# A float32 transformer stack on one core: launch order, last ffn with stationary weights, final norm's gain stored early, two mixer ends reordered

## What is computed

```python
for l in range(DEPTH):
    h = rms_norm(x, norm1_g[l]); proj = h @ w_in[l]          # 1024 -> 3584
    ...
    x = x + jnp.concatenate([ret, sb], axis=-1) @ w_out[l]
    h = rms_norm(x, norm2_g[l])
    x = x + (jax.nn.silu(h @ w_gate[l]) * (h @ w_up[l])) @ w_down[l]   # 2816 wide
return rms_norm(x, final_g)
```

```python
def ffn_sublayer(s, mod, j, g_pre, g_post, wg, wu, wd):
    y = adaln_in(s, g_pre, mod[..., 3 * j, :, :], mod[..., 3 * j + 1, :, :])
    return adaln_out(s, swiglu(y, wg, wu, wd), g_post, mod[..., 3 * j + 2, :, :], FFN_RES)
```

## Time and profile before

| | |
|---|---|
| median of 3 runs | 2390.13 us (2389.59 to 2390.61) |
| the profiled execution | 2390.28 us |
| its span, first to last instruction | 2388.2 us |
| TensorE busy | 2326.7 us, 97% |
| VectorE, ScalarE, GpSimd busy | 1437.3, 1024.8, 166.5 us |
| mean granted clock of TensorE | 0.993 |
| DMA | 364.31 MB, 153 GB/s |

### The profile page before, as it was taken

How to read it: one execution, slowest core, us unless ns; L and a number is a source line. 1 busy time by engine, 2 the same in 40 slices (tenths; PEclk the granted TensorE clock), 3 DMA queues, 4 the chain that set the end, 5 groups by cost and what they waited for, 6 DMA issues and landing times. The chain is left out here.

```text
span 2388.2 us, 28840 instructions
## 1 busy us (share of the span) xinstructions
PE 2326.7 (97%) x10860; PEld 1887.3 (79%) x10860; DVE 1437.3 (60%) x2175; ACT 1024.8 (43%) x1771; POOL 166.5 (7%) x205
## 2 busy tenths in 40 slices
PE   8999999999999999999999999999999999998998
PEld 7877788777888888877777788887878887776777
DVE  5677765777676733455757674337766346466455
ACT  6554556544632223355545222235222235465444
POOL 1200003000000000022100000001000001410000
PEclk9999999999999999999999999999999999999999
DMA  6556654377555522332114554223676232323554
GB/s 223 180 198 242 227 180 156 112 272 254 188 195 184 185 97 80 106 90 71 53 54 167 203 200 145 89 92 118 219 242 204 87 106 81 114 71 104 193 179 141
DMA packets 119880, 364.31 MB, mean 153 GB/s; under 512 B 12224, under 2 KB 12864, under 8 KB 119744
## 3 DMA queue, kind: packets, MB, share of 16 engines
q1 hardware_dynamic: 117488, 355.62, 43.6%
q0 software_dynamic: 2256, 6.86, 1.2%
HBM read 361.35 MB, written 1.09 MB: 152 GB/s over the span
## 5 line engine op out<-in xcount | busy, mean ns | idle before, releaser
L1763 DVE TENSOR_TENSOR wlo<-raw,whi 128x1024 fp32r<-128x1024 f32 x524 | 643.8, 1233 | 483.3 <-ACT whi L1185 476.8
L1185 ACT CAST whi<-raw 128x1024 fp32r<-128x1024 f32 x524 | 548.7, 1051 | 562.0 <-PE ps L632 547.4
L632 PE MATMUL ps<-whi,xhi 128*128 128x512 f32 x1136 | 463.1, 408 | 8.7 <-ACT xhi L1225 4.5
L632 PE MATMUL ps<-wlo,xhi 128*128 128x512 f32 x1136 | 446.6, 393 | 0.0
L632 PE MATMUL ps<-xhi,whi 128*128 128x512 f32 x960 | 375.7, 391 | 1.4 <-DVE hid L2104 1.4
L632 PE MATMUL ps<-whi,ahi 128*128 128x512 f32 x952 | 375.1, 394 | 1.3 <-DVE wlo L1763 0.8
L632 PE MATMUL ps<-xhi,wlo 128*128 128x512 f32 x960 | 373.7, 389 | 0.0
L632 PE MATMUL ps<-xlo,whi 128*128 128x512 f32 x960 | 373.6, 389 | 0.0
L632 PE MATMUL ps<-wlo,ahi 128*128 128x512 f32 x952 | 372.3, 391 | 0.0
L632 PE MATMUL ps<-whi,xlo 128*128 128x512 f32 x1136 | 338.1, 393 | 0.7 <-DVE xlo L1857 0.7
L632 PE MATMUL ps<-whi,alo 128*128 128x512 f32 x952 | 277.3, 390 | 0.0
(11 more groups left out here) (172 smaller groups left out, 1659.4 us busy)
## 6 DMA issues: line engine op xcount, KB each, us to landing
raw<-in_w SPq DMA_DIRECT2D x524, 512.0 KB, 3.5
mraw<-in_w_mod SPq DMA_DIRECT2D x144, 512.0 KB, 5.0
grow<-gains POOLq DMA_DIRECT2D x11, 512.0 KB, 7.3
x<-in_x SPq DMA_DIRECT2D x2, 512.0 KB, 5.2
x<-in_ctx SPq DMA_DIRECT2D x1, 1024.0 KB, 5.7
out<-x SPq DMA_DIRECT2D x2, 512.0 KB, 2.6
rmask<-in_rmask SPq DMA_DIRECT2D x1, 768.0 KB, 5.3
ws<-in_ws POOLq DMA_DIRECT2D x2, 256.0 KB, 11.8
```

Of the source, the lines that this page charges most:

```text
L632: return nc.tensor.matmul(o, lhsT, rhs, start=start, stop=stop, skip_group_check=True)
L1185: nc.scalar.copy(whi[:, slot, :], raw[:, slot, :]).then_inc(hi_done, 1)
L1763: nc.vector.tensor_tensor(wlo[:, slot, :], raw[:, slot, :], whi[:, slot, :].bitcast(F32), ALU.subtract).then_inc(w_split, 1)
```

## The change

- Launch: TensorE runs nine products of 128 columns on the `ones` tile into bank 7 before it waits for the identity (`warm`), and four after tile 0's transposes. VectorE splits unit 0 before it waits for identity and columns. ScalarE makes the operand of tile 0 right after its square and casts unit 1 between its halves, units 2 and 3 after it, then turns to tile 1.
- Last ffn (sublayer 9): chunks 1 to 10 go across, with 256 activation columns moving. Gate and up part of a pair share one bank of four (`pair_place`).
- Final norm: SP stores the gain column behind the load of unit 16; POOL only loads the row in sublayer 3. VectorE's waits on `gains_stored` count one store less, and one stays only for the second block.
- First block's mixers: `o_copied` and `z_taken` are waited for first, six products on `ones` follow, then the wait for `mix_ready`.
- Mixer 5's end: VectorE's output(19) and output(20) ahead of maxima(22) and maxima(23); the copies of mixed rows (`mix_out2`) ahead of the last weights and exponentials; TensorE's `lead_units` 2 and 3 of the second LEAD tile ahead of gmlp.
- Turn 8 to 9 (`ends_whole`): all tall units first, five products on `ones`, tile 0's transposes, seven more. VectorE and ScalarE sum and square tile 1 ahead of and between the operand's parts; ScalarE norms tile 1's row.

```diff
...
-    return s["kind"] == "ffn" and s["tw"] == 4 and c > 0
+    return s["kind"] == "ffn" and (s["tw"] == 4 or s["i"] == 9) and c > 0
...
+        def pair_place(s, q, part):
+            if s["tw"] == 2:
+                return bank((2, 3, 6, 7)[q % 4], 256 * part, 256 * part + 256)
+            return bank(pair_banks(q)[part])
...
             return s["i"] == 2 * DEPTH - 1 and g == CTX_GROUP
+        def ends_whole(s):
+            return s["kind"] == "mix" and s["tt"] == 2
...
                 count += len(SUBS[s["i"] + 1]["wide"][st])
+                count -= s["tt"] == 4 and st == TRAIL
                 RSTD_AT[s["i"] + 1, st] = count
...
+        GAINS_AT = 16
+        final_stored = sem("final_stored")
         X_AT, count = {}, 0
...
                     load_mod(u - 26)
+                if u == GAINS_AT:
+                    sp.wait_ge(cols_landed, 16)
+                    sp.dma_start(gains[0].rearrange("(k p) -> p k", p=P), cols[:, C_FINAL, :],
+                                 allow_slow_non_contiguous=True).then_inc(final_stored, 16)
                 load_mods(u)
...
                 return nc.tensor.matmul(o, lhsT, rhs, start=start, stop=stop, skip_group_check=True)
+            def warm(times, b):
+                for _ in range(times):
+                    mm(bank(b, 0, P), ones[:, :], ones[:, :], True, True)
...
                             q = 2 * (c - 1) + pair
-                            if k == 0 and q >= 3:
+                            if s["tw"] == 2:
+                                if k == 0 and q >= 4:
+                                    pe.wait_ge(pair_taken, s["pair0"] + q - 3)
+                            elif k == 0 and q >= 3:
                                 pe.wait_ge(pair_taken, s["pair0"] + q - 2)
...
                                 pe.wait_ge(chunk_taken, LEAD4 + TAKEN[s["i"], 0, TRAIL])
-                            for part, b in enumerate(pair_banks(q)):
+                            for part in range(2):
                                 c0 = CH * kk + 256 * part + P * pair
                                 hi, lo = (w[:, slot, c0:c0 + P] for w in (whi, wlo))
-                                mm(bank(b), hi, xhi[:, k, :], k == 0, False)
-                                mm(bank(b), hi, xlo[:, k, :], False, False)
-                                last = mm(bank(b), lo, xhi[:, k, :], False, k == KD - 1)
+                                o, xh, xl = pair_place(s, q, part), xhi[:, k, 0:P * s["tw"]], xlo[:, k, 0:P * s["tw"]]
+                                mm(o, hi, xh, k == 0 and (part == 0 or s["tw"] == 4), False)
+                                mm(o, hi, xl, False, False)
+                                last = mm(o, lo, xh, False, k == KD - 1)
                             if k == KD - 1 and pair == 0:
...
                             transposes_in(s, LEAD)
+                            warm(4, 7)
                         wide_pass(s, c, st)
...
                     pe.wait_ge(chunk_taken, LEAD4 + TAKEN[s["i"], s["chunks"] - 1, st])
-                    if across(s):
+                    if across(s) and s["tw"] == 4:
                         pe.wait_ge(pair_taken, s["pair0"] + 2 * s["chunks"] - 3 + st)
...
                             transposes_in(nxt, LEAD)
-                    elif nxt is not None and st == TRAIL and k == s["k"] - 4 + before_the_end(nxt):
+                    elif nxt is not None and not ends_whole(s) and st == TRAIL and k == s["k"] - 4 + before_the_end(nxt):
                         transposes_in(nxt, LEAD)
...
                         tall_pass(s, nxt, g, st)
+                if ends_whole(s):
+                    warm(5, 7)
+                    transposes_in(nxt, LEAD)
+                    warm(7, 7)
...
                     else:
-                        pe.wait_ge(mix_ready, n["mix"] + 4)
                         pe.wait_ge(o_copied, 8 * l + 8)
...
                         b = b0 + pair
+                        if pair == 0:
+                            warm(6, b)
+                        pe.wait_ge(mix_ready, n["mix"] + 4)
                     for kk in range(2):
...
                         if j == 25:
+                            lead_units(s, 1, (2, 3))
                             gmlp(s, (0, 1), 4)
-                            lead_units(s, 1, (2, 3))
                         if j == 26:
...
+            pe.wait_ge(dve_link, 2)
+            warm(9, 7)
             pe.wait_ge(ident_landed, 16)
...
                     high4(1, f_act, s["f_act0"][st] + 1)
+                    if trail:
+                        square_x(1, X_AT[trail["i"], 1])
+                        split_hi(s["u_wide"] + 3)
+                        act.wait_ge(rstd_ready, RSTD_AT[s["i"], TRAIL])
+                        nc.scalar.activation(rows[:, 1, :], x[:, 1, :], ACT.Copy, scale=rstd[:, 1:2]).then_inc(xn_ready, 1)
+                        n["tr"] += 2
+                        return
+                elif launch:
+                    high4(0, f_ready, s["f0"][st] + 1)
+                    split_hi(s["u_wide"] + 1)
+                    high4(1, f_ready, s["f0"][st] + 2)
+                    n["tr"] += 2
+                    return
                 else:
...
                     return
+                if s is not None and ends_whole(s):
+                    if st == LEAD:
+                        square_y(s, LEAD)
+                        split_hi(nxt["u_wide"])
+                        split_hi(nxt["u_wide"] + 1)
+                        square_x(0, X_AT[s["i"], 0])
+                        square_y(s, TRAIL)
+                    operand_hi(nxt, st, s if st == LEAD else None)
+                    return
                 if s is not None and s["blk"] == 2:
...
                     if st == LEAD:
-                        split_hi(1)
+                        operand_hi(nxt, st, launch=True)
+                        split_hi(2)
+                        split_hi(3)
+                        return
                 elif s["i"] == 2 * DEPTH - 1:
...
                     act.wait_ge(pair_taken, s["pair0"] + q - 1)
-                nc.scalar.activation(pgate[:, pair, :], bank(pair_banks(q)[0]), ACT.Silu).then_inc(pair_silu, 1)
+                nc.scalar.activation(pgate[:, pair, 0:P * s["tw"]], pair_place(s, q, 0), ACT.Silu).then_inc(pair_silu, 1)
...
                     proj_out(s, columns, TRAIL)
+                if mixed is not None:
+                    act.wait_ge(tr_ready, mixed)
+                    mix_out2(s, LEAD, 2, 3)
                 if j < len(jobs):
...
                     step2(s, 22)
-                    step2(s, 23)
-                    act.wait_ge(tr_ready, tr + 2)
-                    mix_out2(s, LEAD, 2, 3)
+                    step2(s, 23, mixed=tr + 2)
                     act.wait_ge(mixT_dve, dve_out + 1)
...
                     last.then_inc(f_ready, 1)
+                    if trail:
+                        add_tile(trail, TRAIL, 0)
                     low4(0)
...
                         split_lo(s["u_wide"] + 1)
+                    if trail:
+                        mean_square(1)
+                        n["rstd"] += 1
                     dve.wait_ge(f_act, s["f_act0"][st] + 1)
...
                     which = c_n1(s["l"]) if s["kind"] == "ret" else c_n2(s["l"])
+                    if launch:
+                        split_lo(s["u_wide"])
+                        dve.wait_ge(ident_landed, 16)
+                        dve.wait_ge(cols_landed, 16)
                     for b in range(2):
...
                                                 ALU.mult).then_inc(f_ready, 1)
-                    if launch:
-                        split_lo(s["u_wide"])
                     low4(0)
...
                     if h == 0:
+                        if between:
+                            normed_tile(s, LEAD, 0)
...
                         split_lo(first)
+                    operand_lo(nxt, st, s if st == LEAD else None)
+                    return
+                if s is not None and ends_whole(s):
+                    if st == LEAD:
+                        out_tile(s, LEAD, 0)
+                        add_tile(s, LEAD, 0)
+                        split_lo(first)
+                        mean_square(0)
+                        out_tile(s, TRAIL, 0, between=True)
                     operand_lo(nxt, st, s if st == LEAD else None)
...
                 dve.wait_ge(pair_silu, s["pair0"] + q + 1)
-                nc.vector.tensor_tensor(hid[:, 2 * c + pair, :], pgate[:, pair, :], bank(pair_banks(q)[1]),
+                nc.vector.tensor_tensor(hid[:, 2 * c + pair, 0:P * s["tw"]], pgate[:, pair, 0:P * s["tw"]], pair_place(s, q, 1),
                                         ALU.mult).then_inc(pair_taken, 1)
...
-                        dve.wait_ge(gains_stored, 16 * n["g"])
+                        if s["blk"] == 2:
+                            dve.wait_ge(gains_stored, 16 * (n["g"] - 1))
                         dve.wait_ge(mod_taken, sum(u < nxt["u_wide"] for u in COLS_AT))
...
```

(27 more changed lines are left out.)

## The result

The changed kernel took a median of **2371.94 us** over 6 runs (2371.59 to 2372.63), against 2390.12 over 6 runs of the kernel before beside it: a ratio of 0.9926, interval 0.9917 to 0.9936. That is 18.2 us faster, where 25.9 were forecast. The time lies at the upper end of the stated range of 2358 to 2372: the median is just inside it, and 0.9926 of the 2390.13 us of the kernel before, 2372.4, is 0.4 outside. The profiled execution took 2371.8 us.

The account below looks back on a forecast made before the run. TensorE was taken as the bound, busy 2326.7 of 2388.2 us. Terms 2.0 + 3.4 + 5.5 + 2.6 + 6.5 + 5.9 = 25.9 came off 2390.3, giving 2364.4 us; range 2358 to 2372.

Parts of the forecast that it names:

- Final norm's row: Second layer's ffn: moving the gain store off POOL removes TensorE's 3.8 us `hrow` wait and 1.7 of half clock; 5.5 us.
- first mixer's end: Mixer 5: outputs ahead of maxima give 0.8, weight units ahead of gmlp fill 1.75 us idle; 2.6 us, bounds 0.8 and 3.9.
- turn: Mixer 8 to last ffn: reordering starts the second stream at 2191.7 instead of 2198.33; 6.5 us, bounds 4.5 and 8.
- Last ffn: Sublayer 9's ten chunks: stationary weights with 256-wide products take 110.8 us instead of 116.65; 5.9 us, bounds 7.3 and 1.1.
- I take 0.115, near the half: Last ffn: assumed step in us of a 256-wide product with its weight load, between bounds 0.114 and 0.12.
- rival 2: Last ffn: the 256-wide step is 0.12, or new waits cost as much; 4.8 us lost, 2369.2; chance 0.13.
- Dummy products: First block's mixed rows: six dummies fill 0.7 us of each stall, preventing half clock behind, 2 x 1.7; 3.4 us.
- rival 1: Mixed rows, launch, turn: dummies do not hold the clock; loses 3.4, 0.8 and 1.7 us, 2370.3; chance 0.17.
- Launch: Kernel start: earlier split starts the first product 1.2 us sooner, dummies give 0.8; 2.0 us, bounds 1.2 and 3.4.
- I cost it at nothing: Launch layer, units 17 to 19: loads behind the moved store cost 0, as casts wait for TensorE; uncovered, up to 5.5.
- rival 3: Launch layer: the early store stalls it as it did the later one; 5.5 us lost, 2369.9; chance 0.10.
- 0.4 off: Turn to last ffn: POOL's gain store comes 6 us earlier and falls on chunk 1's loads, costing 0.4 us.

Follow-up runs that it names:

- the old turn alone: Changed kernel with the old order of the turn to the last ffn, stationary weights kept there: 2378.17 us, ratio 0.9953.
- the repaired version: Changed kernel with gain store behind unit 31, ScalarE's lambda exponential behind chunk 1's first splits, fifth tall unit cast and split earlier in retention layers: 2368.39 us.
- its twin without dummies: The repaired version without the six dummy products ahead of the first block's mixed rows, those at launch and turn kept: 2372.18 us, ratio 0.9925.
- the second profile: The changed kernel measured again without any edit, as baseline of a later series: 2372.41 us, ratio 0.9927.

## Why the prediction missed

- **Final norm's row, first mixer's end, turn: right, with some luck in the sizes.** 5.3 for 5.5, 2.7 for 2.6, 6.7 for 6.5. Undoing the first mixer's edits cost the same 2.7, but its gain by positions was 1.1 in the profile with 10.2 us of half clock. The turn's end came where its chain was worked out; TensorE waits there 0.9 us for a split and 0.9 for a cast, and not at all for tile 1's row.
- **Last ffn: the step that failed is "I take 0.115, near the half".** Half of 0.2275 holds half of the fixed part, but each product pays all of it, 0.013 us, and 480 more products pay it 480 more times: 6.2 us, most of the 7.5 that the removed gate transposes were to give. The argument offered for 0.115 (each step of a pair holds two loads and two products) was wrong: the 0.12 of the only 256-column row of the trace was the number to take, and would have given 115.6 us. This was rival 2, priced at 4.8 lost; 4.4 were.
- **Dummy products: the clock held with them** (1.00 behind both mixed rows in each of the ten profiles that have them there; a step of 0.23 at launch), so rival 1 falls. The ground given was off, though: they fill 1.5 us and not 0.7, and no run shows whether a stall with 1.2 us left would have held. Nor is a short idle time enough by itself: in mixer 5 of two profiles (the old turn alone, and the three repairs) the clock fell at 1187 and 1183 behind idle times of 0.4, 0.6 and 0.4 us. The 1.7 us that rival 1 put on the turn's dummies were nothing. The failed step is that the 1.7 us behind each stall would reach the end. The forecast did not ask what TensorE would need 1.7 us earlier: the fifth tall unit, cast behind ScalarE's copies. The forecast named the next late thing at the turn, and not here. Measured 0.95 for 3.4; shown by the repaired version and by its twin without dummies.
- **Launch: 2.6 gained by the 13th product for a forecast 2.0**, then 1.0 given back at unit 4. Same omission.
- **Early store: "I cost it at nothing" was wrong**, rival 3 partly right. Unit 19's cast was read as waiting for TensorE; but it was unit 17 that came late, 3.3 us, and 0.4 us of it reached TensorE (1.3 in the second profile, 1.0 in the middle one of nine). The Trainium skill, "DMA: Bandwidth & Descriptors" (SWDGE vs HWDGE vs iDMA), has software and hardware queues take turns inside an engine. The traces do not show that this shelters anything: weight loads fall to 37 GB/s beside a store on SP's queue, and to 27 GB/s (2181 to 2187) beside one on POOL's.
- **POOL's last store, "0.4 off"**, was a mis-sized term of the turn: behind the new turn it costs 3.2 us of waiting with moving weights, and with stationary ones, in the changed kernel, nothing in the first profile and 0.5 in the second. The forecast had the parts as independent; this pair is not.
- The sum of two losing rivals was left out of the range. Rival 2 came true together with late splits in three places and part of rival 3, and that is how the time came to lie at 2372 and not below.

## What to carry to other kernels

What these runs show: splitting one wide product into two narrow ones costs the fixed part of a product again, so read a narrow product's step in the trace, don't halve a wide one's. When a stall or a half clock goes, ask at once which operand the engine will want that much sooner, and where its cast and split stand in the queues; here over two thirds of such a gain stayed in a late split. The stores of 4-byte elements slowed the loads beside them on SP's queue and on POOL's: put such a store where the ring has slack for all of its length, and look at it again after each edit that makes its surroundings faster.

## What was new about the hardware

- A product of 256 to 512 fp32r columns steps by its columns at 2.4 GHz plus 0.013 to 0.014 us; 128 columns by 0.111 us; repeating the stationary operand saves nothing.
- Behind a stall of one place and length (2.0 us ahead of the first mixed rows) the clock fell in one run and not in another. Of the six stalls of 1.9 to 2.0 us ahead of the mixed rows read without dummies (two in the kernel before, two each without dummies and in the twin of the repaired version) it fell behind five; with six dummy products and 0.6 us left idle, behind none of twenty.
- A product of float32 `ones` on `ones`, 128 columns, leaves two records, and six of them take 1.50 us at full clock: twice what eight transposes of that width had led the forecast to expect.
- The stores of 1024 4-byte elements read here take 8 to 13 us to land, and 512 KB loads beside them move at 27 to 37 GB/s instead of 203. Why was not tried.
- Half clock near 1200 is in all thirteen profiles, for 3.4, 6.8 or 10.2 us, and near 2077 in some; two profiles of the same program had 3.4 and 10.2 us, with and without the one near 2077.
